# The residual stored ahead of the last feed-forward, and its last update added by accumulating transfers

## What is computed

```python
        h = rms_norm(x, norm_ffn_pre[layer])
        u = h @ w_up[layer].astype(h.dtype)
        u = causal_depthwise_conv(u, ffn_conv_w[layer], ffn_conv_b[layer])
        u_gate, u_val = jnp.split(u, 2, axis=-1)
        f = jax.nn.gelu(u_gate, approximate=True) * u_val
        y = f @ w_down[layer].astype(f.dtype)
        x = x + rms_norm(y, norm_ffn_post[layer])
    return x
```

## Time and profile before

| | us |
|---|---|
| median of 3 runs | 1700.87 (1700.36 to 1701.6) |
| the profiled execution | 1702.98 |
| its span, first to last instruction | 1701.2 |
| TensorE busy in it | 1630.9 (96%) |
| VectorE busy | 1136.2 (67%) |
| ScalarE busy | 558.4 (33%) |
| GpSimd busy | 69.1 (4%) |

### The profile page before, as it was taken

The page is one execution under the profiler, slowest core; times in us unless marked ns, Lnnn a source line. Parts: engine busy times, 40 slices in busy tenths (PEclk is TensorE's granted clock), DMA queues, the critical chain, the costliest instruction groups (busy, mean ns, idle before and its releaser), DMA issues.

```text
span 1701.2 us, 25558 instructions
## 1 busy us (share of the span) xinstructions
PE 1630.9 (96%) x9386; PEld 1432.2 (84%) x9386; DVE 1136.2 (67%) x1551; ACT 558.4 (33%) x719; POOL 69.1 (4%) x69
## 2 busy tenths in 40 slices
PE   7999999799999999979999999999997999999995
PEld 6999999799999988758887888887885788888884
DVE  5334555578888842278899888875455888888324
ACT  4222323432222232243333334467334322222221
POOL 3010000110000000020000000000001100000001
PEclk9999999889999999979999999999998999999998
DMA  4352212212222222312322222212222222222232
GB/s 152 108 164 99 86 50 92 69 63 86 99 86 87 98 99 101 109 50 95 105 87 75 90 90 75 90 62 89 85 99 74 74 96 90 97 99 99 101 109 74
DMA packets 44845, 155.41 MB, mean 91 GB/s; under 512 B 5338, under 2 KB 5850, under 8 KB 44800
## 3 DMA queue, kind: packets, MB, share of 16 engines
q1 hardware_dynamic: 41760, 147.26, 24.9%
q0 software_dynamic: 1312, 4.91, 1.0%
q10 hardware_dynamic: 1728, 2.62, 0.5%
HBM read 152.65 MB, written 6.06 MB: 93 GB/s over the span
## 4 chain that ended last, share of the span: by engine, by line
PE 88%; DVE 9%; ACT 2%; issue 1%; DMA 0%; DVEq 0%; SPq 0%; ACTq 0%
PE ps L400 82%; DVE work L1291 3%; PE ps L627 1%; PE ps L608 1%; DVE res L1036 1%; DVE wlo L979 1%; DVE xl L1007 1%; PE ps L486 1%; DVE tmp L1031 1%; PE ps L615 1%; ACT whi L671 1%; PE ps L570 1%; DVE x2l L1007 0%; PE ps L540 0%; DMA raw<-w_dram 0%
## 5 line engine op out<-in xcount | busy, mean ns | idle before, releaser
L400 PE MATMUL ps<-xh,whi 128*128 128x258 f32 (+2 forms) x2048 | 584.6, 334 | 27.9 <-DVE xl L1007 16.4
L400 PE MATMUL ps<-xh,wlo 128*128 128x258 f32 (+2 forms) x2048 | 574.6, 329 | 0.0
L400 PE MATMUL ps<-xl,whi 128*128 128x258 f32 (+2 forms) x2048 | 574.2, 329 | 0.0
L671 ACT ACTIVATE whi<-raw 128x1024 fp32r<-128x1024 f32 x272 | 287.9, 1059 | 654.3 <-PE ps L400 653.4
L979 DVE TENSOR_TENSOR wlo<-raw,whi 128x1024 fp32r<-128x1024 f32 x270 | 330.1, 1223 | 223.9 <-ACT whi L671 223.2
L400 PEld LDWEIGHTS ps<-xh,whi 128*128 128x128 f32 x2048 | 349.8, 192 | 69.3 <-issue 22.4
L400 PEld LDWEIGHTS ps<-xh,wlo 128*128 128x128 f32 x2048 | 349.1, 191 | 33.5
L400 PEld LDWEIGHTS ps<-xl,whi 128*128 128x128 f32 x2048 | 350.4, 192 | 32.0 <-issue 1.0
L1291 DVE SCALAR_TENSOR_TENSOR work<-cin,vecs,work 128x512 f32<-128x512 f32 x240 | 180.1, 750 | 6.8
L400 PE MATMUL ps<-fl,whi 128*128 128x512 f32 x352 | 136.9, 389 | 0.0
L400 PE MATMUL ps<-fh,wlo 128*128 128x512 f32 x352 | 136.9, 389 | 0.0
(11 more groups left out here) (180 smaller groups left out, 1597.7 us busy)
## 6 DMA issues: line engine op xcount, KB each, us to landing
raw<-w_dram SPq DMA_DIRECT2D x272, 512.0 KB, 3.2
bias_copies_dram<-bias_rows_dram POOLq DMA_DIRECT2D x12, 320.0 KB, 4.1
res<-x_dram SPq DMA_DIRECT2D x8, 264.0 KB, 7.0
bias<-bias_copies_dram ACTq DMA_DIRECT2D x8, 256.0 KB, 2.9
out_dram<-res SPq DMA_DIRECT2D x8, 256.0 KB, 2.0
dftp<-dftp_dram POOLq DMA_DIRECT2D x1, 550.7 KB, 5.2
bias<-bias_copies_dram ACTq DMA_DIRECT2D x4, 128.0 KB, 2.0
vecs<-vec_dram SPq DMA_DIRECT2D x1, 364.0 KB, 7.7
```

The source lines that it names most:

```text
L400: last = pe.matmul(ps[:, 2 * pair + h, 0:b - a], w[:, slot, cols], xx[:, k, a:b], start=start and n == 0, stop=stop and n == 2)
L671: act.activation(whi[:, slot, :], raw[:, slot, :], ACT.Copy).then_inc(w_hi, 1)
```

## The change

The rows of `res` are stored to `out` right after they are final, by GpSimd's queue, behind its squares for "pre2f" and ahead of the second up projection. At the end VectorE multiplies each row of `down` in place by the spread factor, read in PSUM, and GpSimd issues for each row a transfer that adds `down` to what stands in `out`. The copy of the factor to SBUF, GpSimd's four products, VectorE's eight additions to `res` and SyncE's stores are gone. GpSimd waits at the end for the eight adding transfers, and ahead of the first of them for the eight plain stores.

```diff
--- before.py
+++ after.py
@@ -279,6 +279,7 @@
         ln_ready = sem("ln_ready")
         silu_ready = sem("silu_ready")
         stored = sem("stored")
+        res_stored = sem("res_stored")
 
         def vec(name, n):
             return vecs[:, VCOL[name] + n:VCOL[name] + n + 1] if isinstance(n, int) else vecs[:, ds(n + VCOL[name], 1)]
@@ -327,11 +328,6 @@
                     sp.wait_ge(w_split, it * 2 + (s - 1))
                     sp.dma_start(raw[:, s, :], w_in[ds(it * 2 + s, 1)].rearrange("a p c -> (a p) c")) \
                       .then_inc(w_landed[s], 16)
-            for k in range(KD):
-
-                sp.wait_ge(res_ready, 3 * KD + k + 1)
-                sp.dma_start(out[:, k, :], res[:, k, N_META:L1]).then_inc(stored, 16)
-            sp.wait_ge(stored, 16 * KD)
 
 
         @block.gpsimd
@@ -383,10 +379,14 @@
             add_squares_of_res("pre2", SEQ)
             add_squares_of_res("pre2f", SEQ)
 
-            pool.wait_ge(rstd_ready, 6)
-            for k in range(1, KD, 2):
-                pool.tensor_tensor(work[:, k // 2, 0:SEQ], down[:, k, :], rstd[:, 0:SEQ], ALU.mult) \
-                    .then_inc(update_ready, 1)
+            for k in range(KD):
+                pool.wait_ge(res_ready, 2 * KD + k + 1)
+                pool.dma_start(out[:, k, :], res[:, k, N_META:L1]).then_inc(res_stored, 16)
+            pool.wait_ge(res_stored, 16 * KD)
+            for k in range(KD):
+                pool.wait_ge(update_ready, k + 1)
+                pool.dma_start(out[:, k, :], down[:, k, :], accum_op=ALU.add).then_inc(stored, 16)
+            pool.wait_ge(stored, 16 * KD)
 
 
         @block.tensor
@@ -949,7 +949,6 @@
             cut_residual("pre2f", "up2", ACT.Gelu_apprx_tanh, "norm_ffn_pre_2", N_META, L1, lambda k: xh2[:, k, :])
             ffn("up2", "down2", True)
             root("post2f")
-            keep_rstd("post2f")
 
 
         @block.vector
@@ -1008,22 +1007,13 @@
                                          in1=hi_part(k).bitcast(F32), op0=ALU.mult, op1=ALU.subtract) \
                    .then_inc(operand_ready, 1)
 
-            def to_residual(name, src, a, b, r0, cut=None):
+            def to_residual(name, src, a, b, r0, cut):
 
                 width = b - a
                 inverse(name)
                 factor = ps[:, STAT, :]
-                if name == "post2f":
-                    dve.wait_ge(rstd_ready, 6)
-                    factor = rstd[:, 0:SEQ]
-                else:
-                    dve.wait_ge(spread_ready, NTH[name])
+                dve.wait_ge(spread_ready, NTH[name])
                 for k in range(KD):
-                    if name == "post2f" and k % 2:
-                        dve.wait_ge(update_ready, k // 2 + 1)
-                        dve.tensor_tensor(res[:, k, a:b], res[:, k, a:b], work[:, k // 2, 0:width], ALU.add) \
-                           .then_inc(res_ready, 1)
-                        continue
                     if k >= 2:
                         dve.wait_ge(res_ready, r0 + k - 1)
                     row = tmp[:, k % 2, 0:width]
@@ -1034,10 +1024,9 @@
                                                ALU.mult))
                     after_step()
                     dve.tensor_tensor(res[:, k, a:b], res[:, k, a:b], row, ALU.add).then_inc(res_ready, 1)
-                    if cut is not None and k:
+                    if k:
                         cut(k - 1)
-                if cut is not None:
-                    cut(KD - 1)
+                cut(KD - 1)
 
             def scaled(phase, n, slot, dst):
 
@@ -1445,7 +1434,10 @@
                                          lambda k: xl2[:, k, :]))
             inverse("pre2f")
             ffn("up2", "down2", 0, "ffn_conv_w_2", "ffn_conv_b_2", "post2f", "f2")
-            to_residual("post2f", lambda k: down[:, k, :], N_META, L1, 3 * KD)
+            inverse("post2f")
+            dve.wait_ge(spread_ready, NTH["post2f"])
+            for k in range(KD):
+                dve.tensor_tensor(down[:, k, :], down[:, k, :], ps[:, STAT, :], ALU.mult).then_inc(update_ready, 1)
```

## The result

The changed kernel takes **1705.55 us** (median of 12 runs, 1704.07 to 1708.05) against 1700.84 for the kernel before beside it (12 runs): a ratio of 1.0028, 95% interval 1.002 to 1.0036. It is 4.7 us slower. The forecast was 1701.3, with a range of 1695.0 to 1711.0: the range holds the time, but it lies beyond the 3.4 us that I had called "same", in the case to which I gave 0.28.

A forecast was written before the change was run, and what follows sets the result against it. TensorE bounds the kernel (busy 96%), leaving a 15.0 us tail; products, issue, eight transfers of 1.39 us, landing and GpSimd's going on end at 1701.20, plus 0.4 makes 1701.6 against 1701.2: median 1701.3, range 1695.0 to 1711.0.

The forecast's parts named there:

- same: Whole kernel: a time between 1697.5 and 1704.3 us, within 3.4 us of no change; chance 0.45.
- to the span's end: End of program: 0.4 us from the last store's landing to the span's end, kept from the kernel before.
- The price of a transfer: Adding transfers at the end: each costs a store plus a load on the same engines, 0.69 + 0.70 = 1.39 us.
- p: Data time per 256 KB adding transfer at the end, taken as 1.39 us; break-even at 1.34.
- Issue keeps pace: GpSimd at the end: issuing a transfer takes 0.52 us, less than the 0.6 of a product.
- 0.07 from product to issue: GpSimd at the end: the first adding transfer is issued 0.07 us after the first product ends.
- 1.7 from last data to landing: GpSimd's queue at the end: transfers land 1.7 us after their last data, read from one earlier copy.
- The early stores: Eight stores of `res` behind the squares of "pre2f": a weight load could grow by 1.9 us, within 2.0 cover; cost zero.
- VectorE disturbed by GpSimd: Tail of the kernel before: VectorE instructions beside GpSimd's products take 1.63 to 1.75 us instead of 0.68 to 0.69.
- A: Rival on the adding transfers: reads of the target are hidden, p near 0.69, giving 1695.7 us; chance 0.27.
- C: Rival on the adding transfers: they don't overlap, p = 3.0, giving 1712.5 us; chance 0.26.
- the forecast's sign (10): Last adding transfer: landing around 10 us after issue would show the forecast, over 13 C, about 4 A.

The follow-up runs named there:

- e2: Changed kernel with plain stores in place of the adding ones on GpSimd's queue (output lacks the residual): 1697.78 us, tail 11.8.
- e1: Changed kernel with the final wait for the eight adding transfers moved from GpSimd to SyncE: 1703.58 us, tail 18.0.
- e4: Changed kernel with two adding transfers of four rows (8 KB pieces) in place of eight of one row: 1704.37 us, tail 19.3.
- e10: Changed kernel with one adding transfer for all eight rows in 2 KB pieces, after the last product: 1708.12 us (one run), tail 22.0.
- e3: Changed kernel with plain stores from SyncE in place of GpSimd's adding transfers (output lacks the residual): 1693.11 us, tail 7.7.
- e6: Kernel before plus the eight early stores of the residual alone, its end storing all rows again: 1700.54 us, ratio 1.0.
- e7: Kernel before without GpSimd and the factor's copy at the end; VectorE does all products and additions, SyncE stores: 1698.23 us.
- e8: Kernel before with VectorE's products first, GpSimd adding three rows (or two) beside them, VectorE the rest, no adding transfers: 1696.42 us (two: 1697.68).
- e5: Changed kernel with all eight adding transfers held until the eighth product is done: 1709.22 us (one run), tail 24.0.
- e9: Changed kernel with the adding transfers cut into pieces of 1 KB instead of 2 KB: 1709.59 us (one run), tail 20.7.
- e11: Changed kernel with adding transfers for rows 0 to 2 alone; VectorE adds and SyncE stores the rest and waits last: 1699.99 us.

## Why the prediction was right or wrong

The forecast tail was 15.4 us (15.0 and the 0.4 of the sum), the measured one 19.9. Term by term:

| term | forecast | measured | |
|---|---|---|---|
| spread to first product's end | 0.73 | 0.70 | right |
| product's end to issue | 0.07 | 0.57 | mis-sized |
| issue to first data | 1.1 | 1.45 (1685.45 to 1686.9) | |
| data of eight transfers | 11.1 | 13.3 (1686.9 to 1700.2) | mis-sized |
| last data to GpSimd going on | 1.98 | 0.7 | mis-sized |
| to the span's end | 0.4 | 3.2 | **wrong** |

- *The step that failed* is "from the last store's landing to the span's end 0.4 pass now, and I keep them". The 0.4 is SyncE's way out. The last wait moved to GpSimd, whose queue drains for 2.9 us behind it. A hint of it was in the trace of before, and I didn't look for it: there the drain stands beside VectorE's tail.

```profile
L121 POOLq DRAIN  x1: 8441/8441/8441, 1686.9 to 1686.9; - x1
```

  It ends at 1695.3, 1.7 us behind GpSimd's last product (1693.68), where nobody waits for it; its length behind transfers no row of before shows. The step is 2.8 us off (3.2 against 0.4), more than half of the miss of 4.5; e2 has the drain without any add, e1 shows that 1.9 of tail come back when the wait is moved.
- *The price of a transfer*, a store plus a load of the same bytes, was the right mechanism for the steady rate: 200 to 215 GB/s, 1.22 to 1.31 us per 256 KB; with its slow start all the data of e4 and e10 makes 1.36 and 1.39 per 256 KB, where 1.39 was my value. The Trainium skill's two-reads rule ("Collectives: The Full Stack", The bandwidth ceiling) had given 1.33, and the traces agree with it as well. What I had not priced is that eight issues beside the data add a little over 2 us: p came out at 1.66. e2 shows that 8.1 us of the tail are the add's, e4 and e10 which part of that is fixed.
- *Issue keeps pace* was taken from plain transfers at 0.52. An adding one takes 0.89 us (7.14 / 8), more than a product's 0.6, though the starts still follow 0.56 apart. It stayed hidden, because data is slower still; issue over 0.6 was one of the signs that I had named against me, and it came.
- *0.07 from product to issue* was read from a GpSimd computation; a transfer on that queue starts 0.55 after its release (e2), on SyncE's 0.08 (e3). +0.5.
- *1.7 from last data to landing* was misread. The copy did not have the DMA engines to itself: SyncE's weight load was issued at 90.01, and what I took for the end of the copy's data, at 91.1, was a gap. The DMA view of 91.4:93 of the kernel before has the rest of the copy (q0, GpSimd's queue; 80 packets in all) beside the load (q1):

```profile
q1 hardware_dynamic: 84, 0.34, 63.7%
q0 software_dynamic: 22, 0.06, 15.3%
```

  The copy's data ends at about 92.1, 0.7 us ahead of its landing at 92.8, and the changed kernel has 0.6. This misreading made the sum 1.0 us too long (1.3 with GpSimd's going on, 0.28 against 0.1) and hid part of the other errors.
- *The early stores* cost nothing: right, shown by e6, with the landing later by 1.8 us (1.9 forecast) and inside the cover.
- *VectorE disturbed by GpSimd* was read rightly: without GpSimd every instruction takes 0.68 (e7), and e8 shows that products with an operand in PSUM are not disturbed.
- *The rivals.* A, reads hidden, is refuted: the add alone costs 8.1 us (e2). C, transfers that don't overlap (p = 3.0), is refuted too: p is 1.66, under the 1.76 at which it would have made the kernel slower by more than 3.4 us; the last landing, 11.4 us after its issue, lies between the forecast's sign (10) and C's (13). The kernel is slower all the same, by a cause that none of my cases held, the way out of the last wait; the 0.28 for slower rested on another mechanism. That the range holds the time is luck in part: its upper end, 1711.0, came from C, and without the misread 1.0 us the forecast would have been 1700.3, further off.

## What to carry to other kernels

An adding transfer is not a store with a free addition: it took the DMA engines twice as long. It did not pay for the last megabytes of this program, where two VectorE instructions per row cost 1.2 us and an adding transfer 1.4 to 1.7; that it would pay where those engines are idle and nobody waits is a guess that no run here tried. Read who executes the last wait of a program, and what that engine's queue still does behind it. Where two engines share a tail, look first at whether their instructions lengthen each other: here dropping GpSimd (and the copy of the factor) gained 2.5 us, and giving GpSimd work only beside instructions that it doesn't disturb gained 4.7.

## What the runs showed of the hardware that I had not expected

- At the end of the program GpSimd's queue drains for 2.9 us when its last wait was for transfers (changed kernel, e2, e5, e9; 2.4 in e4 and e10, 2.3 in e3), and with the wait on SyncE it still ends 1.5 us behind its last landing (e1; 1.1 in e11). SyncE's drain takes 7 ns.
- Eight adding issues beside their data go with over 2 us more of data time than one or two (13.3 against 10.9 and 11.1), and halving the pieces adds only about 0.5 to that (13.8, e9).
- Plain stores from SyncE beside adding transfers land after 4.2 to 5.0 us instead of 2.0 (e11).
